# Edge steps reordered and interleaved, rotary embedding from an SBUF copy, deferred modulation weights in four buffers of their own

## What is computed

```python
shift, scale, gate = split(silu(cond) @ w_mod + b_mod, 3)        # cond: one row for latents, one for the prompt
h = rms_norm(x, g_pre) * (1 + scale) + shift
(sg_u, sg_v, sg_gate, dq, dk, dv, d_gate, nq, nk, nv, n_gate, f_gate, merge) = split(h @ w_in)
y_sg   = sg_u * (W_s @ rms_norm(sg_v) + b)                        # A, per 128-token chunk
y_diff = (softmax1 - lam * softmax2) @ v, dq and dk after axial rope on latents   # B, 4 heads
y_na   = windowed attention with a learned bias plus context keys # C, 8 heads
y_f    = real 2-D DFT of h per channel group                      # D
mixed  = sum over branches of sigmoid(merge_b) * ((y_b * silu(gate_b)) @ p_b)
x      = x + gate * rms_norm(mixed @ w_out, g_post)
```

## Time and profile before

| what | value |
|---|---|
| time, median of 3 runs | 2116.16 us (2113.1 to 2120.86) |
| profiled execution, its own time | 2114.92 us |
| its span, first to last instruction | 2113.1 us |
| mean granted TensorE clock | 0.976 |
| TensorE (PE) busy | 1972.8 us (93%) |
| DVE busy | 948.2 us (45%) |
| ACT busy | 640.1 us (30%) |
| POOL busy | 606.4 us (29%) |
| chain that ended last, by engine | PE 77%, DVE 14%, issue 3%, DMA 2%, ACT 2%, POOL 1% |

### The profile page before, as it was taken

One profiled execution on the slowest core, in us unless ns is written; L12 is line 12 of the kernel. 1 busy time (PEld: TensorE's weight loads), 2 busy tenths in 40 slices (PEclk: granted clock), 3 DMA queues, 4 the chain that ended last, 5 costly groups with the idle time before them and its releaser, 6 DMA issues.

```text
span 2113.1 us, 30534 instructions
## 1 busy us (share of the span) xinstructions
PE 1972.8 (93%) x12364; PEld 1782.6 (84%) x12364; DVE 948.2 (45%) x1489; ACT 640.1 (30%) x1085; POOL 606.4 (29%) x286
## 2 busy tenths in 40 slices
PE   2798988999999999999978999999999999999998
PEld 0597777889888999899967977888898899989996
DVE  3866478454444564330242233455344555433122
ACT  3421232333343321221343222333243332213121
POOL 2632311223222233233323232222222223313331
PEclk7899999999999999999998999999999999999999
DMA  7234333112121122122322221111222112211231
GB/s 276 80 110 145 102 128 120 51 40 91 64 67 51 61 99 70 44 67 75 125 90 90 75 81 67 37 48 41 80 71 71 51 61 89 71 51 60 80 102 78
DMA packets 50956, 172.13 MB, mean 81 GB/s; under 512 B 6656, under 2 KB 7296, under 8 KB 50816
## 3 DMA queue, kind: packets, MB, share of 16 engines
q1 hardware_dynamic: 40736, 145.55, 20.6%
q10 hardware_dynamic: 10080, 24.63, 3.3%
HBM read 162.82 MB, written 7.34 MB: 81 GB/s over the span
## 4 chain that ended last, share of the span: by engine, by line
PE 77%; DVE 14%; issue 3%; DMA 2%; ACT 2%; POOL 1%; ACTq 0%; DVEq 0%; SPq 0%; POOLq 0%
PE ps L1573 53%; PE ps L1461 4%; PE ps L1463 3%; PE ps L1462 3%; DVE mixed L1032 3%; PE ps L1647 2%; PE ps L1666 2%; DMA raw<-in_wstream 2%; PE ps L1675 1%; PE ps L1685 1%; DVE Pm L1291 1%; DVE qr L1196 1%; DVE nmax L1249 1%; PE ps L1727 1%; DVE rt L1187 1%
## 5 line engine op out<-in xcount | busy, mean ns | idle before, releaser
L701 POOL TENSOR_TENSOR wlo<-raw,whi 128x1024 fp32r<-128x1024 f32 x224 | 560.6, 2503 | 1324.4 <-ACT whi L771 1322.4
L1573 PE MATMUL ps<-bufB,whi 128*128 128x320 f32 x2816 | 540.0, 314 | 7.0 <-DVE vn L1144 4.0
L1573 PE MATMUL ps<-bufA,whi 128*128 128x320 f32 x2816 | 540.9, 314 | 2.6 <-DVE z L1411 1.4
L1573 PEld LDWEIGHTS ps<-bufB,whi 128*128 128x128 f32 x2816 | 441.7, 189 | 16.9 <-issue 11.9
L1573 PEld LDWEIGHTS ps<-bufA,whi 128*128 128x128 f32 x2816 | 442.4, 189 | 12.7 <-issue 7.8
L1573 PE MATMUL ps<-bufB,wlo 128*128 128x320 f32 x1408 | 322.7, 310 | 0.0
L1573 PE MATMUL ps<-bufA,wlo 128*128 128x320 f32 x1408 | 322.6, 310 | 0.0
L771 ACT ACTIVATE whi<-raw 128x1024 fp32r<-128x1024 f32 x224 | 237.4, 1060 | 267.2 <-PE ps L1573 120.1
L1573 PEld LDWEIGHTS ps<-bufA,wlo 128*128 128x128 f32 x1408 | 237.3, 189 | 0.0
L1573 PEld LDWEIGHTS ps<-bufB,wlo 128*128 128x128 f32 x1408 | 237.1, 189 | 0.0
L952 ACT ACTIVATE Pm<-ps,nmax 128x640 f32<-128x640 f32 (+2 forms) x160 | 100.0, 625 | 367.2 <-DVE nmax L1249 329.4
(11 more groups left out here) (206 smaller groups left out, 1954.1 us busy)
## 6 DMA issues: line engine op xcount, KB each, us to landing
raw<-in_wstream SPq DMA_DIRECT2D x256, 512.0 KB, 3.3
stage<-in_w_mod SPq DMA_DIRECT2D x16, 512.0 KB, 15.4
out_y_sample<-X ACTq DMA_DIRECT2D x8, 512.0 KB, 2.7
Pm<-in_rpb ACTq DMA_DIRECT2D x12, 256.0 KB, 2.8
X<-in_x_sample SPq DMA_DIRECT2D x4, 512.0 KB, 12.5
xres<-in_x_sample ACTq DMA_DIRECT2D x4, 512.0 KB, 5.3
xres<-out_y_sample ACTq DMA_DIRECT2D x4, 512.0 KB, 5.5
tabs<-in_dft ACTq DMA_DIRECT2D x2, 965.5 KB, 4.6
```

The costliest lines, as they stand in the source:

```text
L701: pool.tensor_tensor(wlo[:, s % SPLITS, :], raw[:, PLAN.entry["W", s] % RAWS, :], whi[:, s % SPLITS, :].bitcast(F32), ALU.subtract).then_i ...
L1573: ins = pe.matmul(ps[:, 2 * b + n, 0:HALF], wt[:, cols], src[:, part, base + k, n * HALF:(n + 1) * HALF], start=k == 0 and wt is hi and pa ...
```

## The change

- **Start.** The two condition rows are loaded first, on the SP queue. All five `XS` come first on ACT, then the new step `ZC` (copy of the first modulation row), then `Xa` and `Xb`, and `Xb` is now DVE's. The low part of h becomes a step of its own, `HL`, on DVE instead of POOL: `DK k, HK k, HL k-1, TK k-2`.
- **Deferred modulation.** The 32 entries get four buffers of their own (`aside`), 4 KB a partition each. They lie in the parts of the projection operand (`bufB`) that nothing uses until the differential attention writes its operand (`YT diff 0`). `raw` holds weights alone, and a `DM` entry waits for the `DM` four before it. The first one waits for the 24 dot products of the start, since the buffers overlap `stage`. SP still issues all of them from one list. The `DM` steps are spread anew: 11 in branch A, 6 in `T dq`, 5 between `T dk` and `T dv`, and 10 in the differential attention, one behind each unit's second `S`.
- **Rotary embedding.** ACT copies the PSUM banks of `T dq 3` and `T dk 3` to SBUF (`plain`), which frees them. DVE computes from the copy.
- **Branch C.** `F nv` comes before `F nk`.
- **Boundary.** `Ya j` and `Xa j-1` before `H j-2`, `HL j-2` behind `Xb j-1`. The slot of `T sgv 3` and those behind it are not split before `T sgv 0 2` (`floor`).

The core of the diff:

```diff
@@ layer_middle
-        s += [("F", "sgg", f)] + some(1) + [("F", "sgu", f), ("SG", f)] + some(1)
+        s += [("F", "sgg", f)] + some(1) + [("F", "sgu", f)] + some(1) + [("SG", f)] + some(f < 3)
...
-        s += [t] + (some(1) if t[2] < 3 else [])
+        s += [t] + (some(2) if t[2] < 3 else [])
...
-        if step[0] == "S" and n < before:
+        if step[0] == "S" and step[6] and n < before:
             s += some(1)
@@ plan
-    for j in range(TILES):
-        add(0, ("XS", j), ("Xa", j), ("Xb", j))
+    add(0, *[("XS", j) for j in range(TILES)], ("ZC",), ("Xa", 0))
+    for j in range(1, TILES):
+        add(0, ("Xa", j), ("Xb", j - 1))
+    add(0, ("Xb", TILES - 1))
     for k in range(KT):
         add(0, ("DK", k), ("HK", k))
+        if k:
+            add(0, ("HL", k - 1))
...
-            if j >= 2:
-                add(l + 1, ("H", j - 2))
             add(l, ("Ya", j))
             if j:
                 add(l + 1, ("Xa", j - 1))
+            if j >= 2:
+                add(l + 1, ("H", j - 2))
             add(l, ("Yb", j))
-            add(l + 1, ("XS", j))
             if j:
                 add(l + 1, ("Xb", j - 1))
+            if j >= 2:
+                add(l + 1, ("HL", j - 2))
+            add(l + 1, ("XS", j))
@@ Plan.__init__
+            if self.layer[self.first_of_slot[n]] and self.steps[self.first_of_slot[n]] == ("T", "sgv", 3, 0):
+                floor = self.at[1, ("T", "sgv", 0, 2)]
+            self.issue.setdefault(max(i, floor), []).append(n)
@@ program
+        staging = stage1[:].rearrange("p a c -> p (a c)")
+        aside = [staging[:, at:at + SLOT] for half in (4 * NTOK, 12 * NTOK) for at in (half, half + SLOT)]
...
+                kind, n = PLAN.stream[e]
+                if kind == "W":
+                    if n >= RAWS:
+                        sp.wait_ge(sems["lo"], n - RAWS + 1)
+                    sp.dma_start(raw[:, n % RAWS, :], A["wstream"][e]).then_inc(sems[f"raw{n % RAWS}"], 16)
+                    return
+                if n >= ASIDE:
+                    sp.wait_ge(sems["dmod"], 2 * (n - ASIDE + 1))
+                elif n == 0:
+                    sp.wait_ge(sems["modrow"], 1)
+                    sp.wait_ge(sems["moddot"], 2 * len(FIRST))
+                sp.dma_start(aside[n % ASIDE], A["wstream"][e]).then_inc(sems[f"dload{n % ASIDE}"], 16)
@@ scalar
+                    elif kind == "T" and step[1] in ("dq", "dk") and step[2] == 3:
+                        for j in range(TILES):
...
+                            act_e.wait_ge(sems["tready"], count.step("tready", k=j + 1))
+                            act_e.activation(plain[:, j, :] if j < 4 else qr[:, 4, :], ps[:, j, :], ACT.Copy).then_inc(sems["tfree"], 1)
@@ vector
+                    elif kind == "HL":
+                        k = step[1]
+                        dve.wait_ge(sems["hhi"], count.step("hhi", ("HK", k)))
+                        dve.tensor_tensor(hT[:, 1, k, :], hz[k % 2][:, 0:NTOK], hT[:, 0, k, :].bitcast(F32), ALU.subtract).then_inc(sems["hlo"], 1)
```

More of the change, by code:

```diff
@@ L272, in layer_middle @@
         if f < 3:
-            between += [("F", n, f + 1) for n in ("nq", "nk", "nv")] + [("VT", f + 1)]
+            between += [("F", n, f + 1) for n in ("nq", "nv", "nk")] + [("VT", f + 1)]
         between += [("F", "ngate", f)]
@@ L440, in __init__ @@
             for n in made:
-                assert all(self.at[0, ("DM", d)] <= i for kind, d in self.stream[:max(self.entry["W", n] - RAWS + 1, 0)] if kind == "D")
+                assert all(self.at[0, ("DM", d - ASIDE)] <= i for kind, d in self.stream[:self.entry["W", n]] if kind == "D" and d >= ASIDE)
         self.unit = {(s[0], s[1], s[2]): s for s in self.steps if s[0] in ("S", "TP", "PV")}
@@ L660, in _ @@
         def _(sp):
+            for c, n in enumerate(("c_row", "ctx_row")):
+                sp.dma_start(rows[:, c, :], A[n].partition_broadcast(P)).then_inc(sems["crow"], 16)
             for j in range(4):
@@ L731, in _ @@
                     power(stats[:, YST, 1, j:j + 1], stats[:, YST, 0, j:j + 1])
[L732 to L737, removed]
                 elif kind == "NR" and step[3] == 1:
@@ L764, in high @@
                 def high(s):
-                    e = PLAN.entry["W", s]
-                    act_e.wait_ge(sems[f"raw{e % RAWS}"], 16 * (e // RAWS + 1))
+                    act_e.wait_ge(sems[f"raw{s % RAWS}"], 16 * (s // RAWS + 1))
                     if s >= SPLITS:
@@ L802, in _ @@
                         squares(X[:, j, :], spare if layer == 0 else junk[:], ss[:, 0, j:j + 1])
-                    elif kind == "Xb" and layer == 0:
-                        j = step[1]
-                        act_e.wait_ge(sems["powd"], count.step("powd", ("Xa", j)))
-                        act_e.activation(X[:, j, :], X[:, j, :], ACT.Copy, scale=stats[:, XST, 1, j:j + 1]).then_inc(sems["xn"], 1)
-                        act_e.wait_ge(sems["xn"], count.own("xn"))
+                    elif kind == "ZC":
+                        act_e.wait_ge(sems["modrow"], 1)
+                        act_e.activation(z[0:2, 0:512], ps[0:2, 7, :], ACT.Copy).then_inc(sems["modcopied"], 1)
+                        act_e.wait_ge(sems["modcopied"], 1)
                     elif kind == "H":
@@ L814, in _ @@
                         if j >= 2:
-                            act_e.wait_ge(sems["hlo"], count.step("hlo", ("H", j - 2)))
+                            act_e.wait_ge(sems["hlo"], count.step("hlo", ("HL", j - 2)))
                         act_e.wait_ge(sems["htp"], count.step("htp", k=1))
@@ L829, in _ @@
                         if k >= 2:
-                            act_e.wait_ge(sems["hlo"], count.step("hlo", ("HK", k - 2)))
+                            act_e.wait_ge(sems["hlo"], count.step("hlo", ("HL", k - 2)))
                         act_e.wait_ge(sems["htp"], count.step("htp"))
@@ L1070, in _ @@
                         n = step[1]
-                        e = PLAN.entry["D", n]
-                        dve.wait_ge(sems[f"raw{e % RAWS}"], 16 * (e // RAWS + 1))
-                        for ins in dots(2 * KT + n, raw[:, e % RAWS, :]):
+                        dve.wait_ge(sems[f"dload{n % ASIDE}"], 16 * (n // ASIDE + 1))
+                        for ins in dots(2 * KT + n, aside[n % ASIDE]):
                             ins.then_inc(sems["dmod"], 1)
@@ L1157, in _ @@
                         for j in range(TILES):
-                            dve.wait_ge(sems["tready"], count.step("tready", k=j + 1))
-                            src = ps[:, j, :]
+                            if name in ("dq", "dk"):
+                                dve.wait_ge(sems["tfree"], count.step("tfree", k=j + 1))
+                                src = plain[:, min(j, 3), :]
+                            else:
+                                dve.wait_ge(sems["tready"], count.step("tready", k=j + 1))
+                                src = ps[:, j, :]
                             if name == "dv":
@@ L1506, in _ @@
                         kt = step[1]
-                        pe.wait_ge(sems["hlo"], count.step("hlo", ("HK", kt)))
+                        pe.wait_ge(sems["hlo"], count.step("hlo", ("HL", kt)))
                         for j in range(TILES):
@@ L1518, in _ @@
                         if name == "sgv":
-                            pe.wait_ge(sems["hlo"], count.step("hlo", ("H", j)))
+                            pe.wait_ge(sems["hlo"], count.step("hlo", ("HL", j)))
                             if part == 0:
```

70 lines of the change are left out of this document (33 added, 37 removed).

## The result

| what | before | after |
|---|---|---|
| time, median | 2117.03 us (2113.1 to 2120.86, 4 runs) | 2086.95 us (2085.12 to 2089.91, 4 runs) |
| profiled execution, its own time | 2114.92 us | 2089.91 us |
| its span | 2113.1 us | 2087.8 us |
| mean granted TensorE clock | 0.976 | 0.977 |
| PE, DVE, ACT, POOL busy, us | 1972.8, 948.2, 640.1, 606.4 | 1977.0, 965.8, 646.4, 591.4 |

The ratio is 0.9861, 95% interval [0.9842, 0.9881]: 30 us faster, where 53 were forecast, and outside the range given.

The account below looks back on a forecast made before the run. TensorE, busy 93% of the span, was taken as the bound, so only its waits and slow clock could give. 9.6 + 8.5 + 18.6 - 1 + 15.5 + 2 = 53.2 off 2114.9 gave 2062 us, range 2045 to 2080.

Parts of the forecast that it names:

- A: At the start: earlier dot products, with `HK 0` held by the fourth split, save 9.6 us; bounds 4 and 16.
- B: Rotary embedding from ACT's copy frees PSUM banks early and removes four TensorE waits: 8.5 us, bounds 4 and 9.5.
- C: Deferred modulation, layer 0's differential attention: one entry per unit recovers 18.6 of 22.6 us excess over layer 1; bounds 10, 22.6.
- Branch A: In branch A a third deferred entry per feature tile adds DVE collisions: -1 us, at worst -6.
- D: Layer boundary: shorter tile loop, third split and low part moved behind `H 3`, save 15.5 us; bounds 6 and 18.
- E: Branch C: with `F nv` before `F nk`, transposes `VT` no longer wait for ACT's copy: 2 us, bounds 0 and 4.
- Rival 3: Loads: a waiting `DM` load holds the weights behind it in SP's list; C gives 3, 2078 us; chance 0.10.
- Rival 1: Boundary: a critical chain stays before `H 3`; 2071 us, or 2080 with both D and C at lower bounds; chance 0.20.
- Rival 5: DVE becomes the bound: nearly every layer 0 dot product collides, 3.3 us each; 21 us slower, 2137 us; chance 0.02.
- Rivals 2 and 4: 2: all terms at favourable bounds, 2045 us, chance 0.14; 4: rotary chain late, B gives 0, 2070 us, chance 0.06.
- The rule against B: Rotary embedding: DVE products with two SBUF inputs contend with GpSimd reads, so the copy's products would be hit; size in rival 4.

Follow-up runs that it names:

- late-split run: The changed kernel with ACT taking the splits of slots 2 and 3 behind `HK 2` instead of before `HK 0`: 2077.45 us, ratio 0.9812.
- the base: The changed kernel run and profiled again without any edit (its second profile): 2085.83 us, ratio 0.9854 against the kernel before.

## Why the prediction was right in places and wrong as a whole

**A, right.** The steps came out: `HK 0` at 42.27 (forecast 41.6), held by the fourth split; DVE idle from 31.6 to 44.4; the last `DK` done at 85.24 (84.7); the first `F sgg` at 96.10 (about 95). 8.4 of 9.6 us (7.0 in the second profile). The late-split run shows the gap that I named to be the term's limit.

**B, mechanism right, too small.** Layer 1 gave 4.8 where half of B is 4.3. In layer 0 I had put the excess of the wait down to C alone. It belongs to B and C together: without the copy layer 0 loses 8.3 us there, and with the copy but the old modulation it loses 8.4 at `T dq` and gets 1.5 back, while both together had gained 8.4. Each part needs the other, so this gain can't be divided between the terms. The undone copy costs 12.9 us against 8.5, above my upper bound of 9.5.

**C, the step that failed**: "Afterwards one entry follows the combination: 4.1 + 2.6 + at most 2.1 for a collision is under 9.9, and the next unit's second `S` comes later than its maximum." That compares DVE's busy time with the length of a unit, and looks at the second `S`. What ends the wait is the *first* maximum of the next unit, which stands in the list of the order and which I didn't follow. In the trace with the pair moved, the combination ends at 266.69 and the `S` that needs the exponential begins at 271.87. From the start of that maximum to that `S` DVE and ACT need 1.87 us (271.91 to 273.78 in the trace after), so 3.3 us are free; `yb` takes 0.35, a pair in the clear 2.6, which fits by 0.3, and a collided pair 4.6, which is 1.7 late. In the trace after it is 1.65 late (waits of 0.62 and 1.03 us). Where the closing work of a head stands behind `yb` as well, even a pair in the clear is late (a wait of 1.42 us at 342.91), and a collided one costs waits of 4.42 us. Of the 12.3 us of waits in the base, 9.1 stand behind the three pairs with a collision; no run separates the collision from the place.

Second, I counted collisions as rare accidents. They aren't: the split follows the second exponential, so a low part starts about with the combination and runs on into the pair, at three of the ten pairs. Third, I left the clock out of the term; it adds some four tenths to the waits.

The measured worth of the part is 3.7 us in place of 17.6, and the excess of layer 0 stays at 17.9 us, over the 10 that I had named as the sign of being wrong. Moving the pair from behind the second `S` to behind the first recovers 17.3 us, which with the 3.7 is 21.0, between my 18.6 and the ceiling of 22.6, and the excess is then 3.3 us. So the ceiling was about right, and the assumption that the change reaches it was wrong.

**Branch A**, -1.7 against -1: right.

**D, right in size.** 13.2 and 12.4 in the two profiles, 11.7 by the times, against 15.5. The tile period is 6.33 and 6.68 us (1062.93, 1069.26, 1075.94 for the transposes; forecast 6.3), so the loop's 5.9 came. The long wait is not gone but 3.37 us, since the third split was worth 4.3 instead of 5.8 and the rest of ACT's and DVE's chain remains.

**E, wrong but small.** About 0 of 2. The waits at `VT` (3.2 us in six places) are gone after the change and come back with `F nk` first, as I had said, but the time doesn't move: two waits of 0.5 us for ACT's `KTt` and somewhat longer ones for `Pm` stand in their place, and what else takes up the gain the runs don't show.

**The rivals.** Rival 3 has nearly the right number for C (3 us) and the wrong cause: the loads part well, and with shared buffers the differential attention loses 3 us at most. Rival 1 came true in kind, with 3.4 us of the chain left, but not in size. Rival 5, DVE's collisions with POOL, was a true mechanism, taken as all or nothing; it should have stood inside C as a term of three collisions and what waits behind them, not beside it with a chance of 0.02. Rivals 2 and 4 did not occur.

**The rule against B.** The first rotary product, 691 to 693 ns before in all 16 cases, now has two SBUF inputs:

```profile
L1208 DVE TENSOR_TENSOR rt<-plain,ropeC x16: 691/693/2792, 190.0 to 1244.0; 128x512 f32<-128x512 f32 x16
L1215 DVE TENSOR_TENSOR rt<-plain,ropeS x32: 424/425/2505, 190.7 to 1245.1; 128x256 f32<-128x256 f32 x32
```

By the Trainium skill, *SBUF — State Buffer*, section "Who interferes with whom", a DVE instruction with two SBUF inputs and a GpSimd instruction that reads SBUF block one another, and the later of the two waits until the first is through. The trace agrees: the products take up to 2792 ns, and the dot product that starts 0.25 us behind a low part of 2.47 us takes 2.1 us more. It took little of the copy's gain, since TensorE then waited only once for this chain, 1.53 us.

## What to carry to other kernels

When side work is woven into an attention, don't ask whether the engine has room in a unit. Ask which instruction behind it ends a wait of TensorE, and how long the engine has up to that one; put the work behind the instruction that others wait for. See also what else starts at the same moment on an engine that slows it, as POOL's low part did here (3.31 us for 1.23), and add the slow clock behind each wait to its price.

## What was not expected of the hardware

- Short waits in the attention cost some 1.4 times their length in the one pair of profiles that shows it: 10.0 us of waits gave 14.0 us when removed, the rest being time at 1.2 GHz behind them (0.51 granted for 6.9 us behind waits of 0.62 and 1.03 us).
- Dot products that met POOL's low part took 3.3 us instead of 1.23. Placed behind the combination, where both follow the second exponential, 3 of 18 did; behind the first maximum none of 16.
- The clock's answer to the same wait differs between executions of one program: two profiles of the changed kernel part by 4.8 us, in steps of 1.2 to 1.8 us at seven places, two of them the other way. The same 1.7 us wait was followed by 8 us near 0.57 in one trace and by full speed in another.
